# S5 recurrence over pairs of time steps, with rotation tables doubled by ScalarE and GpSimd

## What is computed

```python
def _s5_mixer(x, w_in, a_re, a_im, log_dt, b_re, b_im, c_re, c_im, d_skip, w_out):
    u = (x @ w_in).astype(f32)
    dt = jnp.exp(log_dt)[:, None]
    mag = jnp.exp(a_re * dt)
    abar_re, abar_im = mag * jnp.cos(a_im * dt), mag * jnp.sin(a_im * dt)
    ...                                    # coef = (abar - 1) / a ;  bbar = coef * b  (complex)
    def step(carry, ub):
        bu_re = jnp.einsum('blgc,gpc->blgp', ub, bbar_re)
        bu_im = jnp.einsum('blgc,gpc->blgp', ub, bbar_im)
        pr, pi, sr, si = lax.associative_scan(_s5_combine, (a_r, a_i, bu_re, bu_im), axis=1)
        ...
        y = jnp.einsum('blgp,gcp->blgc', sr, c_re) - jnp.einsum('blgp,gcp->blgc', si, c_im)
    y = jax.nn.gelu(y + d_skip * u)
    za, zb = jnp.split(y @ w_out, 2, axis=-1)
    return za * jax.nn.sigmoid(zb)
```

## Time and profile before

| | us |
|---|---|
| median of 3 runs | 3239.03 |
| the three runs | 3239.03, 3234.26, 3244.51 |
| profiled execution, its time | 3238.09 |
| its span | 3236.5 |
| S5 loop on DVE, first product to last product | 2349.30 to 2548.93 |

### The profile page before, as it was taken

How to read it: one execution, slowest core, us unless ns; L and a number is a source line. 1 busy time by engine, 2 the same in 40 slices (tenths; PEclk the granted TensorE clock), 3 DMA queues, 4 the chain that set the end, 5 groups by cost and what they waited for, 6 DMA issues and landing times.

```text
span 3236.5 us, 40485 instructions
## 1 busy us (share of the span) xinstructions
PE 2833.3 (88%) x16182; PEld 2062.0 (64%) x16182; DVE 1629.6 (50%) x2116; ACT 901.8 (28%) x1011; POOL 304.3 (9%) x358
## 2 busy tenths in 40 slices
PE   8888999998869999997889999899734599989998
PEld 8786444443865444444878879688612478788787
DVE  7755111113553111113676556765699675557754
ACT  4422110102431110102334434344200144343442
POOL 2000000000000000000020000000488200002000
PEclk9898999999979999999999999899856799999999
DMA  9204999999417999997324554355400145542450
GB/s 301 89 1 156 394 422 422 422 422 331 139 71 314 422 422 422 422 410 272 118 91 148 191 162 142 98 191 183 116 1 0 55 160 189 156 130 79 146 192 26
DMA packets 274114, 681.79 MB, mean 211 GB/s; under 512 B 10984, under 2 KB 207856, under 8 KB 223296
## 3 DMA queue, kind: packets, MB, share of 16 engines
q1 hardware_dynamic: 266080, 639.79, 53.0%
q0 software_dynamic: 7904, 40.19, 3.5%
HBM read 678.88 MB, written 1.05 MB: 210 GB/s over the span
## 4 chain that ended last, share of the span: by engine, by line
PE 57%; DVE 18%; DMA 17%; ACT 2%; issue 2%; POOL 2%; SPq 0%; DVEq 0%; ACTq 0%; POOLq 0%
DMA ring<-moe_w 16%; PE psum L536 10%; PE psum L552 7%; PE psum L1646 7%; PE psum L537 5%; PE psum L325 5%; PE psum L336 5%; PE psum L312 4%; PE psum L1671 2%; DVE ring_r L286 2%; DVE scratch L3058 2%; PE psum L2210 2%; PE psum L1629 1%; DVE scratch L808 1%; DVE h L468 1%
## 5 line engine op out<-in xcount | busy, mean ns | idle before, releaser
L536 PE MATMUL psum<-scratch_r,scratch_r 128*128 128x512 f32 x1408 | 499.1, 399 | 1.7 <-DVE scratch_r L418 1.6
L1646 PE MATMUL psum<-ring,scratch 128*64 128x512 f32 x2016 | 450.2, 595 | 44.3 <-DMA ring<-moe_w 44.3
L537 PE MATMUL psum<-scratch_r,ring_r 128*128 128x256 f32 x1408 | 395.3, 281 | 0.0
L1646 PEld LDWEIGHTS psum<-ring,scratch 128*64 128x64 f32 x2016 | 146.7, 137 | 321.9 <-issue 318.0
L536 PEld LDWEIGHTS psum<-scratch_r,scratch_r 128*128 128x128 f32 x1408 | 264.5, 188 | 70.3 <-DVE scratch_r L418 5.0
L588 DVE TENSOR_TENSOR ring_r<-ring,scratch_r 128x2048 fp32r<-128x2048 f32 x132 | 294.7, 2286 | 19.4 <-ACT scratch_r L581 19.2
L286 DVE TENSOR_TENSOR ring_r<-ring,scratch_r 128x2048 fp32r<-128x2048 f32 x88 | 203.6, 2321 | 173.1 <-ACT scratch_r L281 171.9
L1845 DVE SCALAR_TENSOR_TENSOR hT_r<-psum,small,hT_r 128x512 fp32r<-128x512 f32 x66 | 46.5, 747 | 453.5 <-ACT hT_r L1784 453.5
L537 PEld LDWEIGHTS psum<-scratch_r,ring_r 128*128 128x128 f32 x1408 | 265.9, 189 | 1.4
L581 ACT CAST scratch_r<-ring 128x2048 fp32r<-128x2048 f32 x132 | 247.1, 1912 | 60.4 <-PE psum L552 60.2
L552 PE MATMUL psum<-scratch_r 128*128 128x512 f32 x704 | 225.2, 392 | 0.0
(11 more groups left out here) (512 smaller groups left out, 4925.2 us busy)
## 6 DMA issues: line engine op xcount, KB each, us to landing
ring<-moe_w SPq DMA_DIRECT2D x372, 1024.0 KB, 20.7
ring<-ffn_w_gate_up SPq DMA_DIRECT2D x88, 1024.0 KB, 5.1
ring<-ffn_w_down SPq DMA_DIRECT2D x44, 1024.0 KB, 4.8
ring<-hgrn_w_in SPq DMA_DIRECT2D x32, 1024.0 KB, 5.5
scratch<-moe_w POOLq DMA_DIRECT2D x24, 1024.0 KB, 10.8
ring<-a_w_in SPq DMA_DIRECT2D x16, 1024.0 KB, 12.4
ring<-mlstm_w_in SPq DMA_DIRECT2D x12, 1024.0 KB, 5.3
ring<-kv_w SPq DMA_DIRECT2D x8, 1024.0 KB, 11.9
```

The source lines that it names most:

```text
L536: pe.matmul(bank, w[0][:, j, fc], both[:, :, j, :], start=(j == 0), stop=False)
L537: mm = pe.matmul(bank[:, 0:T], w[1][:, j, fc], both[:, 0, j, :], start=False, stop=(j == KT - 1))
L1646: mm = pe.matmul(psum[c, k, :], xg[:, j, c], ws[x][:, i, k, :], start=(j == 0), stop=(j == KT - 1))
```

## The change

Every second time step only is kept in the scan (`CHUNK = 2`, `S5_K` = 128 pairs).

- PE multiplies the even inputs with a B and the odd ones with B, into the same 128 columns (4 matmuls a tile where there were 2 of double length). `s5_BT_a` (a B) is a third set of 16 transposes; ACT writes u with even and odd steps apart.
- y at odd steps is C times the pair's state. y at even steps is Re(C a s) of the pair before plus Re(C B) u, for which there are `s5_CT_a` (a C, 6 DVE instructions of 1024) and `lag0` (64 small matmuls, PE, once, and a copy by ACT). Each q has 20 y matmuls of 127 or 128 columns.
- Scan factor is mag². All DVE instructions of the loop have half the elements, the scans too; turning back sums up on DVE (5 instructions where there were 3), so PE gets 2 terms instead of 4.
- The tables have 128 steps: 3 doubling levels a q instead of 4. The products of a level are ACT's: for each of 4 tiles two activations with a per-partition scale (`turns(q)`), the sums stay with POOL (two `tensor_tensor` a level). The two alternate through `s5_turned` and `s5_table`.

Extracts from the diff (the rest are the buffers' new places and the same edits of shapes):

```diff
@@ s5_pe
+                    for r in range(2):
+                        e.matmul(bank[rows_, S5_K:T], s5_CT[:, r * KT + q, rows_], w[:, r, j, :],
+                                 start=(r == 0), stop=(r == 1))
+                    e.matmul(bank[rows_, 0:S5_K], s5_lag0[rows_, q, :], u8[rows_, q, 0, :], start=True, stop=False)
+                    for r in range(2):
+                        mm = e.matmul(bank[rows_, 1:S5_K], s5_CT_a[:, r * KT + q, rows_], w[:, r, j, 0:S5_K - 1],
+                                      start=False, stop=(r == 1))
...
+                if q == 0:
+                    lag0()
+                if q == 1:
+                    pe.wait_ge(*taken("s5", "lag0"))
@@ s5_act
+            def turns(q):
+
+                tab = s5_tab[q % 2]
+                for i, k in enumerate(range(S5_DOUBLED, 7)):
+                    n = 1 << k
+                    act.wait_ge(sem("s5_table"), (8 - S5_DOUBLED) * q + i + 1)
+                    for j in range(QT):
+                        m = QT * q + j
+                        a.activation(tab[:, :, j, n:2 * n], tab[:, :, j, 0:n], ACT.Copy, scale=s5_pow[:, 0, k + 1, m:m + 1])
+                        last = a.activation(s5_pt[:, :, j, 0:n], tab[:, :, j, 0:n], ACT.Copy, scale=s5_pow[:, 1, k + 1, m:m + 1])
+                        if j < QT - 1:
+                            last.then_inc(act_step, 1)
+                            act.wait_ge(act_step, act_steps.next())
+                    last.then_inc(sem("s5_turned"), 1)
+                    act.wait_ge(sem("s5_turned"), done("s5_turned"))
+
+            for name, dst in (("bTa", s5_BT_a), ("cT", s5_CT), ("bT", s5_BT)):
+                if name == "bT":
+                    turns(0)
                 for i in range(4):
...
+            act.wait_ge(psum_ready, job("s5", "lag0"))
+            a.copy(s5_lag0, bank_of("s5", "lag0")[:, 0:32 * KT].rearrange("p (q c) -> p q c", q=KT)).then_inc(act_took, 1)
+            act.wait_ge(act_took, act_reads.next())
             for q in range(KT):
+                if q + 1 < KT:
+                    turns(q + 1)
                 act.wait_ge(*taken("s5", "y", q))
                 x = s5_y[:, T * q:T * (q + 1)]
                 a.activation(x, x, ACT.Gelu_apprx_tanh).then_inc(sem("s5_gelu"), 1)
@@ s5_pool
+                for k in range(S5_DOUBLED, 7):
+                    n = 1 << k
+                    pool.wait_ge(sem("s5_turned"), done("s5_turned_read"))
+                    for r, op in enumerate((ALU.subtract, ALU.add)):
+                        x = tab[:, r, :, n:2 * n]
+                        last = g.tensor_tensor(x, x, s5_pt[:, 1 - r, :, 0:n], op)
...
+                    last.then_inc(sem("s5_table"), 1)
@@ s5_dve
-                dve.wait_ge(sem("s5_table"), q + 1)
+                dve.wait_ge(sem("s5_table"), (8 - S5_DOUBLED) * (q + 1))
...
-                v.scalar_tensor_tensor(out=g2[:, 1, :], in0=g2[:, 1, :], scalar=-1.0, in1=tab2[:, 1, :],
-                                       op0=ALU.mult, op1=ALU.mult).then_inc(sem("s5_x"), 1)
+                v.tensor_tensor(g2[:, 1, :], g2[:, 1, :], tab2[:, 1, :], ALU.mult).then_inc(dve_step, 1)
+                dve.wait_ge(dve_step, dve_steps.next())
+                v.tensor_tensor(w2[:, 1, :], w2[:, 1, :], g2[:, 0, :], ALU.add).then_inc(dve_step, 1)
+                dve.wait_ge(dve_step, dve_steps.next())
+                v.tensor_tensor(w2[:, 0, :], w2[:, 0, :], g2[:, 1, :], ALU.subtract).then_inc(sem("s5_x"), 1)
```

More of the change, by code:

```diff
@@ L2756, in s5_pe @@
             c16 = scr(5).rearrange("p (m n) -> p m n", n=P)
-            for name, src in (("bT", b16), ("cT", c16)):
-                pe.wait_ge(sem("s5_bcT"), 1 if name == "bT" else 2)
+            for k, (name, src) in enumerate((("bTa", b16), ("cT", c16), ("bT", b16))):
+                pe.wait_ge(sem("s5_bcT"), k + 1)
                 for i in range(4):
@@ L2860, in double @@
                 n = 1 << k
-                pc, ps = (bc(s5_pow[:, r, k, tiles], [P, tiles.stop - tiles.start, n]) for r in range(2))
+                pc, ps = (bc(s5_pow[:, r, k + 1, tiles], [P, tiles.stop - tiles.start, n]) for r in range(2))
                 c0, s0 = tab[:, 0, :, 0:n], tab[:, 1, :, 0:n]
@@ L2892, in s5_pool @@
                 for r in range(2):
-                    g.tensor_copy(tab[:, r, :, 0:S5_BASE], s5_base[min(q, 1)][:, r, tiles, :]).then_inc(pool_step, 1)
-                    pool.wait_ge(pool_step, pool_steps.next())
-                for k in range(S5_DOUBLED, 8):
-                    last = double(tab, s5_pt[min(q, 1)], k, tiles)
-                    if k < 7:
+                    last = g.tensor_copy(tab[:, r, :, 0:S5_BASE], s5_base[:, r, tiles, :])
+                    if r == 0:
                         last.then_inc(pool_step, 1)
@@ L2901, in s5_pool @@
                 pool.wait_ge(sem("s5_table"), done("s5_table"))
+                for k in range(S5_DOUBLED, 7):
[4 more added lines that the diff above has]
+                        last = g.tensor_tensor(x, x, s5_pt[:, 1 - r, :, 0:n], op)
+                        if r == 0:
+                            last.then_inc(pool_step, 1)
+                            pool.wait_ge(pool_step, pool_steps.next())
+                    last.then_inc(sem("s5_table"), 1)
+                    pool.wait_ge(sem("s5_table"), done("s5_table"))
         def s5_dve(dve):
@@ L2991, in s5_dve @@
                 dve.wait_ge(dve_step, dve_steps.next())
+            for dst, x, y, op in ((car, cr, ci, ALU.subtract), (cai, ci, cr, ALU.add)):
+                v.tensor_tensor(dst, x, ar, ALU.mult).then_inc(dve_step, 1)
+                dve.wait_ge(dve_step, dve_steps.next())
+                v.tensor_tensor(tmp, y, ai, ALU.mult).then_inc(dve_step, 1)
+                dve.wait_ge(dve_step, dve_steps.next())
+                v.tensor_tensor(dst, dst, tmp, op).then_inc(dve_step, 1)
+                dve.wait_ge(dve_step, dve_steps.next())
             v.memset(scr(3), 0.0).then_inc(dve_step, 1)
@@ L3019, in s5_dve @@
             dve.wait_ge(sem("s5_bcT"), done("s5_bcT"))
+            dve.wait_ge(psum_ready, job("s5", "bTa", 3))
+            b_tiles(cr, ci)
+            dve.wait_ge(psum_ready, job("s5", "cT", 3))
+            dve.wait_ge(*taken("s5", "cT", 3))
+            sh = [P, S5_TILES, 2 * S5_C]
+            for r, op in enumerate((ALU.add, ALU.subtract)):
+                v.tensor_tensor(s5_Ca_tiles[:, r, :, :], s5_C_tiles[:, r, :, :], bc(ar, sh), ALU.mult).then_inc(dve_step, 1)
+                dve.wait_ge(dve_step, dve_steps.next())
+                v.tensor_tensor(s5_Ca_tmp, s5_C_tiles[:, 1 - r, :, :], bc(ai, sh), ALU.mult).then_inc(dve_step, 1)
+                dve.wait_ge(dve_step, dve_steps.next())
+                v.tensor_tensor(s5_Ca_tiles[:, r, :, :], s5_Ca_tiles[:, r, :, :], s5_Ca_tmp, op).then_inc(dve_step, 1)
+                dve.wait_ge(dve_step, dve_steps.next())
             def y_of(q):
```

108 lines of the change are left out of this document (65 added, 43 removed).

## The result

| | median us | lowest to highest, runs | ratio to before, 95% interval |
|---|---|---|---|
| kernel before | 3236.31 | 3232.29 to 3244.51, 8 | |
| changed kernel | 3228.80 | 3224.97 to 3230.48, 8 | 0.9973, 0.9963 to 0.9984 |

What follows compares the result with a forecast made beforehand. The prediction took the chain of DVE's eight q turns and PE's last y as the bound. Last product -3.2 and last y -2 gave -5.2 on the profiled 3238.09 us: 3232.9, so a median of 3234 us, range 3221 to 3252.

Steps and rivals of the forecast that it cites:

- DVE's turn: DVE's work for one q of the S5 loop, halved by the change: 13.5 us if POOL is idle.
- one exposed table, y's end to first product: DVE's wait for a table from q = 2 on: Gelu, copy, ACT's activations, POOL's sums and hand-overs, 12.6 us.
- period: Time of one q in the S5 loop, DVE's work plus the exposed table: 26.1 us, against 25.75 before.
- first product: Start of the S5 loop, after table 0 and four copies of B by ACT: at 2352 us, before 2349.3.
- first to second turn: From loop start until table 1 is ready, behind ACT's copy of `lag0`: 22.8 us, to 2374.8.
- end of the last product: End of DVE's last product in the S5 loop: 2545.7 us, before 2548.9, a saving of 3.2.
- last y: PE's y matmuls behind DVE's last product, for which all wait: 4.6 us in place of 6.63, saving 2.
- The reading of the order: `turns(q+1)` stands in ACT's stream behind a Gelu waiting for DVE's y of q-1, so tables 2 to 7 are exposed.
- two of POOL's levels 1.7: In the start, POOL's sums for two levels of table 0, within `turns(0)`: 1.7 us.
- with narrower weights I take 0.07: PE's `lag0` matmuls before table 1: 0.07 us for each of 128 records, 9 us; ends 6 and 28 us.
- 62% of the columns: Scaling of PE's closing y by columns: 4.1 of 6.63 us, 4.6 with more weight loads.
- Rival (c): The tables are hidden after all beside DVE's work: 9.4 us gained on each of six tables, 3178 us; chance 0.03.

Runs made afterwards that it cites:

- e1_order: The changed kernel with one edit: ACT makes table q+2, not q+1, ahead of the Gelu of q; 3161.9 us, 0.9771 of the kernel before.
- e4_lag_together: The changed kernel with each y's matmuls in three passes over the column groups (C, `lag0`, a C), not group by group; 3223.1 us, 0.9957 of the kernel before.

## Why the forecast held, and where its steps were off

By the profiles, each link beside what the forecast gave:

| step | forecast | measured |
|---|---|---|
| DVE's turn | 13.5 | 13.43 |
| one exposed table, y's end to first product | 12.6 | 12.25 |
| period | 26.1 | 25.68 |
| first product | 2352 | 2356.64 |
| first to second turn | 22.8 | 17.63 |
| start of turn 2 | 2402.2 | 2401.29 |
| end of the last product | 2545.7 | 2542.62 |
| last y | 4.6 | 7.3 |
| profiled execution | 3232.9 | 3230.16 |

**The reading of the order was right**, and e1_order shows it: the same work, one place earlier in ACT's stream, is worth 67 us. The pause begins with Gelu, is ended by POOL and is 1.8 us longer the first time (13.58 for 11.79): Gelu's table load of 1.28 us lies on the path, and no `low_of` of half a microsecond stands ahead of the pause yet.

**The turn and the table's price were right**, both from rows of other stages. The lengths of ACT's activations, 0.32, 0.35 and 0.40, came out as the line through the earlier trace rows had them; in pairs with one wait they take 2.2, 2.4 and 2.9 us a level (forecast 2.3, 2.6 and 3.0), POOL's sums 3.2 as forecast. The 24 lengths sum to 8.4 us, against 8.6 forecast from the rows and 6.0 by the table in the Trainium skill, "VectorE: DVE Perf Modes", section on the TRN2 errata: the row was the better guide. The Trainium skill has a closer figure on another page, "ScalarE: Activation LUTs", section "What ACT_TABLE_LOAD costs": 186 ns and 0.833 ns an element, about 93 ns more for a per-partition pointer, and 93 ns of overlap. By it the lengths are 0.31, 0.33 and 0.39, and the trace agrees within 0.02.

**The start was 4.6 us too early.** The step that failed is "two of POOL's levels 1.7": they took 2.41 and 2.62, since DVE's a C, which the forecast had taken only as something hidden, ran at the same time. I had priced contention in the loop and not here. That made the end of `turns(0)` 2.8 us late. The rest is in PE: its first `bu` took 2.2 us and not 0.5.

**`lag0` was 7 us too dear.** The step "with narrower weights I take 0.07" a record gave 9 us. PE's timeline of the changed kernel:

```profile
2359.49 2.01 PE L2805 MATMUL psum<-scratch 128*32 128x32 f32 x128
```

That is 0.016 a record, under the lower end of 0.05. The rows it was taken from were of matmuls over all columns of the array, one after the other; these change the column group after each two matmuls and overlap. That the two errors cancelled is luck: turn 2 began 0.9 us before the forecast. The time alone would have told of neither.

**The last y was 2.7 us too short.** The step "62% of the columns" scales with columns, and the last y isn't bound by them. Read record by record, the last y of the kernel before has 20 steps, of 0.43 us each while the clock is 0.50 and 0.22 after. The changed kernel's has 20 of C and a C with half the columns (0.21), and on top eight steps of `lag0` and eight changes of operand rows at 0.14 us (e4_lag_together above). The rule of the Trainium skill, "TensorEngine Tiling (Array Packing)", section "Key Properties", that a change of the mode drains the engine, fits a price for each change. The clock is the other half of the miss: 6.63 was measured at a mean granted clock of 0.68, the last y of the changed kernel ran at 0.50. The first 16 records of the y before took some 4.3 us at 0.50, so all 32 would take some 8.6 there, and 62% of that is 5.4: an estimate, 1.3 over the 4.1 that the forecast started from. The changes add 1.1, and `lag0`, which shares its steps with nothing, about 0.6 over its columns; the forecast had allowed 0.5 for all of it. A run that has the changes alone was not made; the 0.14 is read from the distances of the records.

**Rival (c)**, had the change hidden its tables, was put at 3178 us. With the order mended the kernel takes 3161.9, 16 us less: DVE loses 0.9 us a turn beside POOL and not 3.2, because POOL's work a turn is a fifth of what it was (4.2 us in e1_order, 21.3 before) and mostly falls beside instructions that it doesn't slow.

From the stage come 5.1 us of the gain, as the table has it (forecast 5.2). The medians differ by 7.5; the remaining 2.4 us are within the interval of the ratio, some 3.4 us either way.

## What to carry to other kernels

When work is moved to an engine that also serves the end of a turn, look at what stands ahead of it in that engine's stream: behind an instruction that waits for this turn's result, it cannot be hidden, however many buffers there are and however idle the engine is. Compute ahead by as many turns as there are buffers (here q+2 for q+1: 67 us). And give small matmuls of different column groups to PE one after another, with all that have the same number of rows together: the last y went from 7.3 to 2.7 us with the same 40 records, 3.8 of it by the groups side by side and 0.8 by the fewer changes of rows.

## What the runs showed of the hardware that I had not expected

- Matmuls on different groups of 32 columns run side by side, with fp32 operands: 16 records of 128 columns in 1.10 us at a granted clock of 0.50, and 128 records of 32 columns in 2.01 us.
- A change between 128-row and 32-row operands cost 0.14 to 0.18 us beyond the step of 0.21 from one record to the next, at a granted clock of 0.50.
- A short operation on POOL beside long ones of DVE can last as long as they do: two sums of 64 elements took 2.41 us beside two instructions of 1024 elements, the second ending 0.17 us after the second of DVE's, and 0.71 with DVE idle. In the loop two sums of 256 took 2.24 in place of 1.52, and DVE lost 0.8.
- ACT's copies of u, with even and odd columns written apart, took 1.05 us where the plain copies of the same 128x512 took 0.58. It costs little here, as ACT waits for PE between them (4.71 us before the last).
- A wait of ACT on its own last instruction costs 0.14 us, nine times a table.
- PE's granted clock was 0.50 throughout the changed loop, with PE busy for 81 of 148 us, and a mean of 0.64 before, with 57 of 148: more busy time did not bring more of the higher level.
